# Six raw-weight slots in the MLP, and a third k pair in seven block products in the first pair of chunks of three down stages

## What is computed

```python
z = rmsnorm(h, norm2_w) @ mlp_w1          # 2048 -> 8192
h = h + jnp.square(jax.nn.relu(z)) @ mlp_w2   # 8192 -> 2048
```

## Time and profile before

| | us |
|---|---|
| median of 3 runs (2035.07 to 2035.69) | 2035.51 |
| the profiled execution | 2033.51 |
| its span, first to last instruction | 2031.7 |
| PE busy | 2017.1 (99%) |
| DVE busy | 1499.1 (74%) |
| ACT busy | 1281.3 (63%) |

### The profile page before, as it was taken

One profiled execution on the slowest core, in us unless ns is written; L12 is line 12 of the kernel. 1 busy time (PEld: TensorE's weight loads), 2 busy tenths in 40 slices (PEclk: granted clock), 3 DMA queues, 4 the chain that ended last, 5 costly groups with the idle time before them and its releaser, 6 DMA issues.

```text
span 2031.7 us, 25864 instructions
## 1 busy us (share of the span) xinstructions
PE 2017.1 (99%) x9829; PEld 1701.9 (84%) x9829; DVE 1499.1 (74%) x2020; ACT 1281.3 (63%) x1898; POOL 6.1 (0%) x12
## 2 busy tenths in 40 slices
PE   9999999999999999999999999999999999999998
PEld 7888888888898888887889988888888888888886
DVE  6666565788977777788967557877886886797664
ACT  7666666656566688656566445577647746755754
POOL 0000000000000000000000000000000000000000
PEclk9999999999999999999999999999999999999999
DMA  8766555555655555565655556666666565666664
GB/s 263 210 191 196 168 155 158 181 189 177 201 174 184 175 158 149 184 201 168 204 159 156 146 147 194 191 184 199 195 208 196 184 215 182 189 196 204 209 206 146
DMA packets 194784, 375.49 MB, mean 185 GB/s; under 512 B 13875, under 2 KB 48917, under 8 KB 194134
## 3 DMA queue, kind: packets, MB, share of 16 engines
q1 hardware_dynamic: 194662, 373.85, 59.7%
HBM read 371.71 MB, written 2.10 MB: 184 GB/s over the span
## 4 chain that ended last, share of the span: by engine, by line
PE 64%; DVE 3%; ACT 1%; DMA 1%; issue 0%; ACTq 0%; DVEq 0%
PE acc L630 14%; PE acc L632 14%; PE acc L631 14%; PE acc L821 3%; PE acc L823 3%; PE acc L824 3%; PE acc L1143 2%; PE acc L1145 2%; PE acc L1144 2%; PE acc L988 1%; DVE wlo L1956 1%; PE acc L966 1%; PE tp L642 1%; PE tp L988 1%; PE xb L998 1%; DMA raw<-in_mlp_w 1%
## 5 line engine op out<-in xcount | busy, mean ns | idle before, releaser
L1956 DVE TENSOR_TENSOR wlo<-raw,whi 128x1024 fp32r<-128x1024 f32 x612 | 739.9, 1221 | 332.4 <-ACT whi L1330 328.9
L1330 ACT ACTIVATE whi<-raw 128x1024 fp32r<-128x1024 f32 x612 | 644.2, 1058 | 474.9 <-PE acc L632 309.0
L630 PE MATMUL acc<-whi,both 128*128 128x512 f32 (+1 forms) x592 | 226.8, 383 | 0.3 <-DVE wlo L1961 0.3
L632 PE MATMUL acc<-whi,both 128*128 128x512 f32 (+1 forms) x592 | 224.6, 379 | 0.0
L631 PE MATMUL acc<-wlo,both 128*128 128x512 f32 (+1 forms) x592 | 224.4, 379 | 0.0
L630 PE MATMUL acc<-whi,aT 128*128 128x512 f32 x508 | 200.1, 394 | 0.0
L630 PE MATMUL acc<-whi,bT 128*128 128x512 f32 x512 | 199.2, 389 | 0.0
L631 PE MATMUL acc<-wlo,bT 128*128 128x512 f32 x512 | 199.2, 389 | 0.0
L632 PE MATMUL acc<-whi,bT 128*128 128x512 f32 x512 | 199.2, 389 | 0.0
L632 PE MATMUL acc<-whi,aT 128*128 128x512 f32 x508 | 198.1, 390 | 0.0
L631 PE MATMUL acc<-wlo,aT 128*128 128x512 f32 x508 | 197.8, 389 | 0.0
(11 more groups left out here) (518 smaller groups left out, 3815.0 us busy)
## 6 DMA issues: line engine op xcount, KB each, us to landing
raw<-in_mlp_w SPq DMA_DIRECT2D x256, 512.0 KB, 4.2
raw<-in_w_in_a SPq DMA_DIRECT2D x128, 512.0 KB, 3.9
raw<-in_w_ple_gate SPq DMA_DIRECT2D x64, 512.0 KB, 4.0
raw<-in_w_in SPq DMA_DIRECT2D x64, 512.0 KB, 3.8
raw<-in_w_in_b SPq DMA_DIRECT2D x40, 512.0 KB, 4.2
raw<-in_w_out_a SPq DMA_DIRECT2D x32, 512.0 KB, 3.9
raw<-in_w_out_b SPq DMA_DIRECT2D x32, 512.0 KB, 4.4
raw<-in_w_out SPq DMA_DIRECT2D x32, 512.0 KB, 4.4
```

Source lines behind the costliest of these rows:

```text
L630: pe.matmul(o, hi[:, kt, tok], whi[:, slot, wc], start=start, stop=False)
L632: mm = pe.matmul(o, lo[:, kt, tok], whi[:, slot, wc], start=False, stop=stop)
L1330: act.activation(whi[:, u % RING, 0:n], raw[:, u % RING, 0:n], ACT.Copy).then_inc(hi_done, 1)
L1956: dve.tensor_tensor(wlo[:, u % RING, 0:n], raw[:, u % RING, 0:n], whi[:, u % RING, 0:n].bitcast(F32), ALU.subtract).then_inc(lo_done, 1)
```

## The change

- `FAST[0]` goes from (3, 5) to (1, 3, 5). k pair 1 (units 2 and 3) of the first pair of chunks is now in seven block products too, in the stages down0, down1 and down2.
- From up0 to down2 the raw ring has `DEEP` = 6 slots. Slots 4 and 5 lie in a tile `more`, over the free end of `nat` and the second half of `r3`, where one of the two `first` tiles lay. A unit's load waits for the `lo_done` of the slot's last user (`raw_free`), which is the unit six earlier. `whi` and `wlo` stay at four.
- There is one tile `first`. The ACT copy into it goes from step 11 to step 13 of its pair, and waits for the `tokens_added` of the pair before (`pair_x`).
- SP waits for `pool_split` ahead of up0, and for the last user of slot 5 ahead of the load of the final gains.

```diff
+DEEP = 6
-FAST = ((3, 5), (1, 3, 5))
+FAST = ((1, 3, 5), (1, 3, 5))
...
-        first = [sb(f"first{i}", [P, 2, CH], F32, (r3 + 4 * KB, tab_at + 4 * KB)[i]) for i in range(2)]
+        first = sb("first", [P, 2, CH], F32, tab_at + 4 * KB)
+        apart = (r3 - nat_at - 8 * KB) // (2 * KB)
+        more = sb("more", [P, apart + 2, CH], F32, nat_at + 12 * KB)
...
+        def slot_of(u):
+            return (u - S["up0"].u0) % DEEP if S["up0"].u0 <= u < S[f"up{PAIRED}"].u0 else u % RING
+
+        held, raw_free, raw_counts = [[] for _ in range(DEEP)], [], []
+        for u in range(units):
+            users = held[slot_of(u)]
+            raw_free.append(users[-1] + 1 if users else 0)
+            users.append(u)
+            raw_counts.append(16 * len(users))
...
                 if u >= RING or not isinstance(r, int):
-                    sp.wait_ge(lo_done, u - RING + 1 + r)
-                dst = raw[:, u % RING, 0:s.kt * s.cols].rearrange("p (k n) -> p k n", k=s.kt)
-                sp.dma_start(dst, unit_source(s, j, uu)).then_inc(raw_full[u % RING], 16)
+                    sp.wait_ge(lo_done, raw_free[u] + r)
+                dst = raw_of(u, 0, s.kt * s.cols).rearrange("p (k n) -> p k n", k=s.kt)
+                sp.dma_start(dst, unit_source(s, j, uu)).then_inc(raw_full[slot_of(u)], 16)
...
             for b in range(DFF // D):
+                if b == 0:
+                    sp.wait_ge(sem("pool_split"), 4)
                 stage(f"up{b}")
                 if b == PAIRED:
+                    sp.wait_ge(lo_done, held[DEEP - 1][-1] + 1)
...
                 act.wait_ge(unit_used, u + 1)
-                if n >= len(OUT_PAIRS) + 2:
-                    act.wait_ge(sem("pair_x"), 2 * (n - len(OUT_PAIRS) - 1))
+                if n > len(OUT_PAIRS):
+                    act.wait_ge(sem("pair_x"), 2 * (n - len(OUT_PAIRS)))
...
                     uu = 2 * FAST[j][-1]
-                    along(s, j, join({} if j else z_hi(q, 3), {uu + 1: [lambda n=2 * q + j, u=s.u0 + j * s.units + uu: first_product_out(len(OUT_PAIRS) + n, u)]}))
+                    along(s, j, join({} if j else z_hi(q, 3), {uu + 3: [lambda n=2 * q + j, u=s.u0 + j * s.units + uu: first_product_out(len(OUT_PAIRS) + n, u)]}))
```

More of the change, by code:

```diff
@@ L317, in sem @@
             return sems[name]
-        raw_full = [sem(f"raw_full{i}") for i in range(RING)]
+        raw_full = [sem(f"raw_full{i}") for i in range(DEEP)]
         hi_done, lo_done = sem("hi_done"), sem("lo_done")
@@ L383, in shared_of @@
         def shared_of(n):
-            return (out_first, out_second) if n < len(OUT_PAIRS) else (first[n % 2], second)
+            return (out_first, out_second) if n < len(OUT_PAIRS) else (first, second)
         def sums_due(u, after):
@@ L404, in quarters @@
         def quarters(u):
-            return raw[:, u % RING:u % RING + 2, :].rearrange("p s (i n) -> p (s i) n", n=CH)
+            slot = slot_of(u)
+            if slot < RING:
+                return raw[:, slot:slot + 2, :].rearrange("p s (i n) -> p (s i) n", n=CH), (0, 1, 2, 3)
+            return more, (0, 1, apart, apart + 1)
         def norm_at(u):
@@ L426, in build, with raw_of @@
         V0 = 2 * GKW
-        def raw_count(u):
-            return 16 * (u // RING + 1)
+        def slot_of(u):
[6 more added lines that the diff above has]
+            raw_counts.append(16 * len(users))
+        def raw_count(u):
+            return raw_counts[u]
+        def raw_of(u, lo, hi):
+            slot = slot_of(u)
+            if slot < RING:
+                return raw[:, slot, lo:hi]
+            return more[:, (0, apart)[slot - RING]:, :].rearrange("p i n -> p (i n)")[:, lo:hi]
         def unit_source(s, j, uu):
@@ L1316, in split_to @@
                     kt, cols = shape_of(u)
-                    act.wait_ge(raw_full[u % RING], raw_count(u) + r * 16 // RING if isinstance(r, int) else raw_count(u) + r * (16 // RING))
+                    act.wait_ge(raw_full[slot_of(u)], raw_count(u) + r * 16 // RING if isinstance(r, int) else raw_count(u) + r * (16 // RING))
                     if u >= RING:
@@ L1323, in split_to @@
                     if f and f[1] == 0:
-                        act.activation(whi[:, u % RING, 0:CH], raw[:, u % RING, 0:CH], ACT.Copy).then_inc(hi_done, 1)
+                        act.activation(whi[:, u % RING, 0:CH], raw_of(u, 0, CH), ACT.Copy).then_inc(hi_done, 1)
                     elif cols == 2 * QHEAD:
@@ L1329, in split_to @@
                     elif g is None:
-                        act.activation(whi[:, u % RING, 0:n], raw[:, u % RING, 0:n], ACT.Copy).then_inc(hi_done, 1)
+                        act.activation(whi[:, u % RING, 0:n], raw_of(u, 0, n), ACT.Copy).then_inc(hi_done, 1)
                     else:
@@ L1946, in split_to @@
                         dve.wait_ge(hi_done, u + 1)
-                        dve.tensor_tensor(wlo[:, u % RING, 0:CH], raw[:, u % RING, 0:CH], whi[:, u % RING, 0:CH].bitcast(F32), ALU.subtract).then_inc(lo_done, 1)
+                        dve.tensor_tensor(wlo[:, u % RING, 0:CH], raw_of(u, 0, CH), whi[:, u % RING, 0:CH].bitcast(F32), ALU.subtract).then_inc(lo_done, 1)
                         continue
@@ L1955, in split_to @@
                     elif g is None:
-                        dve.tensor_tensor(wlo[:, u % RING, 0:n], raw[:, u % RING, 0:n], whi[:, u % RING, 0:n].bitcast(F32),
+                        dve.tensor_tensor(wlo[:, u % RING, 0:n], raw_of(u, 0, n), whi[:, u % RING, 0:n].bitcast(F32),
                                           ALU.subtract).then_inc(lo_done, 1)
@@ L1990, in quad_summed @@
             def quad_summed(u, g):
-                sums, four = quads(g)[0], quarters(u)
+                sums, (four, at) = quads(g)[0], quarters(u)
                 if g >= 2:
@@ L1995, in quad_summed @@
                 for v in (u, u + 1):
-                    dve.wait_ge(raw_full[v % RING], raw_count(v))
-                dve.tensor_tensor(sums[:, 0:2, :], four[:, 0:4:3, :], four[:, 1:2, :].to_broadcast((P, 2, CH)), ALU.add).then_inc(sem("quad_step"), 1)
+                    dve.wait_ge(raw_full[slot_of(v)], raw_count(v))
+                dve.tensor_tensor(sums[:, 0:2, :], four[:, 0:at[3] + 1:at[3], :], four[:, 1:2, :].to_broadcast((P, 2, CH)), ALU.add).then_inc(sem("quad_step"), 1)
                 dve.wait_ge(sem("quad_step"), 2 * g + 1)
-                dve.tensor_tensor(sums[:, 2, :], sums[:, 0, :], four[:, 3, :], ALU.add).then_inc(sem("quad_step"), 1)
+                dve.tensor_tensor(sums[:, 2, :], sums[:, 0, :], four[:, at[3], :], ALU.add).then_inc(sem("quad_step"), 1)
                 dve.wait_ge(sem("quad_step"), 2 * g + 2)
-                dve.tensor_tensor(sums[:, 3, :], sums[:, 2, :], four[:, 2, :], ALU.add).then_inc(sem("quad_sums"), 1)
+                dve.tensor_tensor(sums[:, 3, :], sums[:, 2, :], four[:, at[2], :], ALU.add).then_inc(sem("quad_sums"), 1)
             def quad_split(g):
```

## The result

The changed kernel takes 2049.19 us (median of 4, 2048.80 to 2050.68) against 2035.60 for the kernel before on the same chip: ratio 1.0073, with a 95% interval of 1.0061 to 1.0085. It is 13.6 us slower by the medians, and 14.9 by the ratio (0.73%). The direction was forecast, the size was not: 2041.9 with a range to 2045.5. In the profiles the span went from 2031.7 to 2047.0 us, + 15.3.

A forecast was written before the change was run, and what follows sets the result against it. PE, 99% busy at full clock, was taken to bound the kernel. New seam waits +11.2, old waits gone -2.8, matmuls removed -2.04 sum to +6.4 us: 2041.9 us, range 2036.5 to 2045.5.

The forecast's parts named there:

- The step by step sum of the seam: First pair of each down stage: PE waits at units 4 to 7, 3.73 us lost per stage, 11.2 in three.
- The additions ahead of the up chunk's transposes: DVE's three new additions, 2.70 us, fit in 2.08 idle plus 0.5 from the half split: no cost.
- Unit 12's waits: Old PE waits in down0 to down2, 0.38, 0.52 and 0.65 us plus restarts; forecast to go, margin 0.5.
- 2.8: PE's old waits at units 7 and 12 with restarts, in us over three down stages; forecast to fall away whole.
- 2.04: PE work removed in the three down stages: 9 matmuls at 0.2267, in us, all saved on the path.
- Six slots: no cost: Loads start two units earlier, removing ACT's and DVE's DMA waits; gain at most unit 12's share, already counted.
- SP's new wait: SP waits for `pool_split`, work done in out2's first chunk, three chunks ahead of its use: zero cost.
- if the up stages wait: One of the listed signs that would show the forecast wrong: waits in the up stages.
- the fourth rival: PE's clock falls behind the new 2.2 us wait: +3 to +10 us on top; 2%.
- The first and second rivals: First: slots caused the repeating bubble, 2030.7, 6%. Second: supply catches up at unit 6, 2034.9, 13%.
- The third: Up chunk's transposes pushed later or unit 12's margin fails: +8 to +14, 2044 to 2049; 9%.
- The rule on repeated gaps: Same gap repeating on the engine that should be saturated can mean too few buffers; would give the first rival's 2030.7.

The follow-up runs named there:

- both waits mended: Changed kernel with the first stage's register-loop load wait put back to four units earlier and the six slots numbered from 2 on: 2041.35 us, ratio 1.0033.
- first mended: Changed kernel with only the first stage's register-loop load wait put back to the unit four earlier: 2042.82 us, ratio 1.0040.
- products alone: Kernel before, four slots, with only k pair 1 of the first pair of chunks in seven block products too: 2043.87 us, ratio 1.0043.
- ACT's bands moved: Kernel with both waits mended, plus ACT's two bands at the seam moved from steps 0 and 1 to 2 and 4: 2036.12 us, ratio 1.0004.
- slots alone: Kernel with both waits mended, but the first pair's k pairs (3, 5) as before: 2032.84 us, ratio 0.9990.

## Why the prediction was right and wrong

**Right: what bounds, what is saved, what the seam costs.** The step by step sum of the seam (units 4 to 7 late by 0.61, 0.35, 2.31 and 0.46 with restarts, 3.73 us per stage) was measured at 3.67. The additions ahead of the up chunk's transposes cost nothing, as said: their idle time before shrank from 2.08 to 1.21 us. Unit 12's waits went. 3 x 3.67 - 2.8 - 2.04 is 6.2, the profiles have 6.4 from T on. That the kernel with both waits mended comes out at 2041.35, so near the 2041.9 of the forecast, is in part luck: its median holds about one fall of the clock, some 1.5 us, that the sum doesn't have.

**Wrong: the step "Six slots: no cost".** It named two things the edit does, the earlier load and SP's new wait, and priced both rightly at nothing or a gain. It took "the slot's last user is the unit six earlier" for the whole of the new expression, and so put its cost at zero. The runs show 6.7 us (by medians) to 8.1 (by ratio) in its place, the profiles 8.6. Two places where the expression says something else were not looked at: the register loop, where the expression is evaluated for chunk 0 and used for all (5.3 to 6.8 us in the runs, 7.7 in the profiles, half of the loss), and the seam of the two numberings (0.9). Both were in the diff, in the line with `else 0` and in `slot_of`; neither shows in the order of instructions, which moves nothing there. Writing out both expressions for the eight units of one later chunk would have shown the wait of units 0 to 2; its price would still have been an estimate, since the seven starts cost from 0.2 to over 2 us each. With the measured terms the sum is 6.4 + 7.7 + 0.9 = 15.0, where the profiles have 15.3. The forecast's own list of signs held this one: wrong "if the up stages wait", and up0 did.

**Undersized: the fourth rival.** I gave the clock 2%, since no slice of the trace before showed a fall. But no matmul in that trace's MLP was over 0.6 us late, and its two waits of 1.5 us elsewhere are shorter than the new one of 2.2. Behind waits of 1.5 and 2.2 us it fell in five of the fifteen places that profiles show (both waits mended, first mended, products alone, ACT's bands moved, the changed kernel itself), and behind 4.0 us in three of three. It isn't part of the profiled 15.3, but of the medians of the mended kernels, and by their clocks (0.998, 0.998, 0.997) of the other three executions of the changed kernel.

**The first and second rivals** are out: slots alone leave unit 7's wait as it was, and with the products the waits are the same with four slots and with six. The third named 2044 to 2049, next to what was measured, but by another way: the transposes of the up chunk weren't pushed later than the forecast had them, and unit 12 didn't wait. Its number came near by luck.

**The rule on repeated gaps** of the Trainium skill ("Perfetto Trace Analysis", section Optimization Strategy) would have given 2030.7. The runs show one of the two gaps to be of that kind (1.65 us by medians, 1.4 in the trace); the larger gain came from moving work of two engines by a few steps.

## What to carry to other kernels

When a wait's threshold changes from a formula to a table, work it out for the cases at the edges: the first units, a loop whose body is written once and run with an offset, and the point where one numbering hands over to another. A seam between stages is won or lost by what stands in program order ahead of the next operand on the engines that feed PE, so write that order down with durations before taking PE's work away, and move what isn't due yet behind what is. A wait of PE of 1.5 to 2 us can cost about as much again in clock behind it, as it did here in some of the executions.

## What the runs showed of the hardware

- Behind waits of PE of 1.5 to 4.0 us the granted clock fell to 0.50 for some six to nine 512-column matmuls, which then start 0.43 us apart and not 0.227. In the first pairs of the down stages it came at 4.0 us in three of three places, at 2.2 us in four of twelve, at 1.5 us in one of three. In the first stage it came behind one of two waits of 2.0 us, and behind the two waits of 1.5 us that each profile has outside the MLP it never came.
- A restart of PE costs 0.08 to 0.11 us beyond the wait, at each of the waits in the down stages where the clock stays up.
- Steps of ACT and DVE repeat so well that a chain of eight of them, written down from another kernel's trace, was met within 0.02 us (unit 4's start, behind a shorter chain, within 0.09).
